# ScalarE reads the decay rate as a scale and takes the decay's square, in the recurrence of the second network

## The reference, cut to what matters

```python
def rg_lru(x, w_r, b_r, w_i, b_i, lam):
    xb = x.reshape(B, S, RNN_BLOCKS, RNN_BLOCK_DIM)
    r = sigmoid(einsum('bsnc,ncd->bsnd', xb, w_r).reshape(B, S, D_RNN) + b_r)
    i = sigmoid(einsum('bsnc,ncd->bsnd', xb, w_i).reshape(B, S, D_RNN) + b_i)
    log_a = -LRU_C * r * softplus(-lam)          # LRU_C = 8
    a = exp(log_a)
    u = sqrt(-expm1(2.0 * log_a)) * (i * x)
    # then h[t] = a[t] * h[t-1] + u[t] along the positions
```

## Time and profile before

| | us |
|---|---|
| median of 3 runs | 2782.74 |
| lowest and highest run | 2771.02, 2784.29 |
| the profiled execution | 2781.65 |
| its span in the profile | 2779.6 |

### The profile page before, as it was taken

The page is one execution under the profiler, slowest core; times in us unless marked ns, Lnnn a source line. Parts: engine busy times, 40 slices in busy tenths (PEclk is TensorE's granted clock), DMA queues, the critical chain, the costliest instruction groups (busy, mean ns, idle before and its releaser), DMA issues. The chain is left out here.

```text
span 2779.6 us, 48273 instructions
## 1 busy us (share of the span) xinstructions
PE 2601.0 (94%) x20505; PEld 2138.3 (77%) x20505; DVE 2017.6 (73%) x2876; ACT 1534.7 (55%) x2217; POOL 128.9 (5%) x176
## 2 busy tenths in 40 slices
PE   8899999998997999999999999998999889999888
PEld 7689987787965666666666666666969779979778
DVE  7755558654356989889898989896757865757864
ACT  5544425221124877777777778775446444546443
POOL 0000000010004000000000000000200101100101
PEclk9999999999997999999999999999999999999999
DMA  6325433100033989899999989893625534625532
GB/s 193 97 73 185 162 117 116 61 4 3 4 135 118 367 331 365 332 347 349 345 351 347 350 330 365 332 365 105 197 74 167 175 104 145 196 76 167 166 105 101
DMA packets 250985, 550.43 MB, mean 198 GB/s; under 512 B 25549, under 2 KB 193157, under 8 KB 207629
## 3 DMA queue, kind: packets, MB, share of 16 engines
q1 hardware_dynamic: 246796, 541.52, 56.1%
q0 software_dynamic: 3968, 5.78, 0.7%
HBM read 540.43 MB, written 1.05 MB: 195 GB/s over the span
## 5 line engine op out<-in xcount | busy, mean ns | idle before, releaser
L316 DVE TENSOR_TENSOR wl<-raw,wh 128x1024 fp32r<-128x1024 f32 (+1 forms) x610 | 742.6, 1221 | 341.8 <-ACT wh L307 324.1
L307 ACT ACTIVATE wh<-raw 128x1024 fp32r<-128x1024 f32 (+1 forms) x610 | 640.5, 1053 | 485.0 <-PE PS L163 434.0
L316 DVE TENSOR_TENSOR wl<-early,wh 128x1024 fp32r<-128x1024 f32 x384 | 466.8, 1225 | 55.6 <-ACT wh L307 35.3
L307 ACT ACTIVATE wh<-early 128x1024 fp32r<-128x1024 f32 x384 | 407.0, 1061 | 128.0 <-PE PS L163 118.7
L161 PE MATMUL PS<-wh,xe_h 128*96 128x512 f32 x896 | 357.2, 399 | 1.2 <-DVE xe_l L2018 1.2
L161 PE MATMUL PS<-b_hn_h,wh 128*128 128x256 f32 (+1 forms) x1152 | 336.9, 292 | 22.1 <-DVE wl L316 15.9
L163 PE MATMUL PS<-wh,xe_l 128*96 128x512 f32 x896 | 353.6, 395 | 0.0
L162 PE MATMUL PS<-wl,xe_h 128*96 128x512 f32 x896 | 353.6, 395 | 0.0
L162 PE MATMUL PS<-b_hn_l,wh 128*128 128x256 f32 (+1 forms) x1152 | 329.6, 286 | 0.0
L163 PE MATMUL PS<-b_hn_h,wl 128*128 128x256 f32 (+1 forms) x1152 | 329.4, 286 | 0.0
L161 PEld LDWEIGHTS PS<-b_hn_h,wh 128*128 128x128 f32 (+1 forms) x1152 | 223.0, 194 | 28.4 <-DVE wl L316 18.3
(11 more groups left out here) (473 smaller groups left out, 5046.8 us busy)
## 6 DMA issues: line engine op xcount, KB each, us to landing
early<-in_moe_in SPq DMA_DIRECT2D x128, 1024.0 KB, 5.0
raw<-in_moe_in SPq DMA_DIRECT2D x96, 1024.0 KB, 4.9
raw<-in_w_in SPq DMA_DIRECT2D x76, 1024.0 KB, 5.4
early<-in_moe_out SPq DMA_DIRECT2D x64, 1024.0 KB, 4.9
raw<-in_moe_out SPq DMA_DIRECT2D x48, 1024.0 KB, 5.0
raw<-in_attn_w_in SPq DMA_DIRECT2D x24, 512.0 KB, 5.8
raw<-in_rw_w_rkv SPq DMA_DIRECT2D x12, 1024.0 KB, 5.0
raw<-in_ffn_w_gate SPq DMA_DIRECT2D x11, 1024.0 KB, 5.5
```

What stands on the lines that cost most here:

```text
L307: act.e.activation(st.two(n)[0], st.raw(n), ACT.Copy).then_inc(*act.sig("hi", st.name, n, sem=f"hi_{st.name}"))
L316: dve.e.tensor_tensor(lo, st.raw(n), hi.bitcast(F32), SUB).then_inc(*dve.sig("lo", st.name, n, sem=f"lo_{st.name}"))
```

## The change

In the stage of bv, VectorE's eight products by the rate are left out. `decays(n)` on ScalarE does the same by its own scale: two exponentials of one block each, with the block's column of nsp as the scale, then two tanh with the column of psp (+8 softplus(-lam), one more small VectorE instruction, put into the scratch column set 4). It waits for the rates and for the gates' eviction. In the stage of mb, the square of the decay moves from VectorE to ScalarE (`squares`), between `high` and the eviction of mb; it waits for its own `decays` and for VectorE's II x CX of the same round, because it overwrites CX. VectorE's `roots_in(n)` comes one round later, behind the next round's II x CX, and the last one after the loop.

```diff
-    nsp = spv[:, 5, :]
+    nsp, psp = spv[:, 5, :], spv[:, 4, :]
@@ second_act
         def decays(n):
+            act.wait_ge(act.at("rates", l))
+            act.wait_ge(act.at("lru", l, 0, 2 * n + 1))
+            for x in (2 * n, 2 * n + 1):
+                e.activation(AA_[:, x, :], RR_[:, x, :], ACT.Exp, scale=nsp[:, x:x + 1]).then_inc(*act.own())
+            act.wait_ge(act.last)
+            for x in (2 * n, 2 * n + 1):
+                e.activation(RR_[:, x, :], RR_[:, x, :], ACT.Tanh, scale=psp[:, x:x + 1]).then_inc(*act.sig("decays", l, n))
+
+        def squares(n):
             c = slice(2 * n, 2 * n + 2)
-            act.wait_ge(act.at("log_a", l, n))
-            e.activation(AA_[:, c, :], RR_[:, c, :], ACT.Exp).then_inc(*act.own())
-            act.wait_ge(act.last)
-            e.activation(RR_[:, c, :], RR_[:, c, :], ACT.Tanh, scale=-1.0).then_inc(*act.sig("decays", l, n))
+            act.wait_ge(act.at("decays", l, n))
+            act.wait_ge(act.at("gated", l, n))
+            e.activation(CX_[:, c, :], AA_[:, c, :], ACT.Square).then_inc(*act.sig("squares", l, n))
...
         for u in range(KC):
             high(act, SB)
+            squares(u)
             taken("mb", u, M[:, u, :], ACT.Sigmoid)
@@ second_dve
-        e.tensor_scalar(nsp_, nsp_, -8.0, None, MUL).then_inc(*dve.own())
+        e.tensor_scalar(psp, nsp_, 8.0, None, MUL)
+        e.tensor_scalar(nsp_, nsp_, -8.0, None, MUL).then_inc(*dve.sig("rates", l))
...
         for u in range(KC):
             low(dve, SB)
-            c = slice(2 * u, 2 * u + 2)
-            dve.wait_ge(dve.at("lru", l, 0, 2 * u + 1))
-            e.tensor_tensor(RR_[:, c, :], RR_[:, c, :], bc(nsp[:, c], [RB, 2, SEQ], 2), MUL).then_inc(*dve.sig("log_a", l, u))
+
+        def roots_in(n):
+            c = slice(2 * n, 2 * n + 2)
+            dve.wait_ge(dve.at("squares", l, n))
+            e.scalar_tensor_tensor(CX_[:, c, :], CX_[:, c, :], 1.0, RR_[:, c, :], ADD, MUL).then_inc(*dve.sig("roots_in", l, n))
+
         for u in range(KC):
             low(dve, SB)
             c = slice(2 * u, 2 * u + 2)
             dve.wait_ge(dve.at("lru", l, 1, NRB - 1))
-            e.tensor_tensor(II_[:, c, :], II_[:, c, :], CX_[:, c, :], MUL).then_inc(*dve.own())
-            dve.wait_ge(dve.at("decays", l, u))
-            dve.wait_ge(dve.last)
-            e.tensor_tensor(CX_[:, c, :], AA_[:, c, :], AA_[:, c, :], MUL).then_inc(*dve.own())
-            dve.wait_ge(dve.last)
-            e.scalar_tensor_tensor(CX_[:, c, :], CX_[:, c, :], 1.0, RR_[:, c, :], ADD, MUL).then_inc(*dve.sig("roots_in", l, u))
+            e.tensor_tensor(II_[:, c, :], II_[:, c, :], CX_[:, c, :], MUL).then_inc(*dve.sig("gated", l, u))
+            if u:
+                roots_in(u - 1)
+        roots_in(KC - 1)
```

More of the change, by code:

```diff
@@ L69 @@
     "route_mm": "by_expert_mm logits_mm ht_mm count_mm rank_mm rows_mm",
-    "b": "iq ik iwt plus plus_exp plus_log xr xr_zero q k iw conv rot spun scored log_a roots_in lru_out rnn_in mb gr ga ma bv lru "
+    "b": "iq ik iwt plus plus_exp plus_log xr xr_zero q k iw conv rot spun scored rates gated squares roots_in lru_out rnn_in mb gr ga ma bv lru "
          "index decays roots",
```

## The result

| | before | after |
|---|---|---|
| median of 8 runs, us | 2781.68 | 2797.19 |
| lowest to highest, us | 2771.02 to 2784.29 | 2793.23 to 2805.89 |
| the profiled execution, us | 2781.65 | 2796.83 |
| its span, us | 2779.6 | 2794.7 |

The ratio is 1.0063, 95% interval 1.0050 to 1.0075: slower, by 15.5 us between the medians.

A forecast was written before the change was run, and what follows sets the result against it. TensorE, busy 94% of the span, was taken as the bound. Layer shifts of 8.8 and 8.1 us, 16.9 together, on the profiled 2781.65 give 2798.5; with 1.1 for the median, 2799.6 us, range 2788 to 2811.

The forecast's parts named there:

- The bound: Whole kernel: TensorE, busy 94% of the span; only what makes it wait, around mb in each layer, moves the time.
- P1 to P9: Weight pieces ScalarE splits, P0 to P7 in mb's eight rounds, P8 and P9 in gr's first; TensorE's 2.86 us each.
- The rate products: bv stretch: removal from VectorE worth nothing; ScalarE's decays 1.73 us, 0.54 more each, 4.3 for eight.
- The lock: mb rounds: ScalarE and VectorE hand over twice a round, 3.74 us against 3.26 before and TensorE's 2.86.
- The sum: Both stretches up to TensorE's start of P9: +8.8 us in layer 1, +8.1 us in layer 2.
- (d): Rival, decays and what follows the stretch: cheaper decays or part of the shift absorbed, 2794.6 us; chance 0.16.
- (a): Rival, mb rounds: they don't lock, TensorE's 4.20 us gap goes, -8.4 in two layers, 2774 us; chance 0.06.
- (b): Rival, mb rounds: Square not in the loaded table set, sigmoids need reloads, 9.7 us a layer, 2819 us; chance 0.04.
- (c): Rival, mb rounds: TensorE's waits drop its clock to 1.2 GHz, 6 us later a layer, 2812 us; chance 0.06.

The follow-up runs named there:

- the experiment: The changed kernel with constants -1 and 1 as the scale of exponentials and tanh in place of rates read from memory: 2794.11 us, ratio 1.0053.

## Why the prediction was right, point by point

**The bound.** The dates that I took as the ones that matter, TensorE's at P1 to P9, are where it waits after the change (all but P2 in layer 1). The parts of the program outside of the two stretches differ between the two executions by 2.3 us at most, and that is ahead of the first stretch.

**The rate products.** Taking them from VectorE was worth nothing, as said: in the regular rounds of bv in layer 1 it stood for ScalarE's high part before (0.3 or 0.8 us) and stands longer now (1.5 or 2.0). Their price on ScalarE was 4.23 us to P0 where I had 4.1, and 3.67 in layer 2 where I had 3.4: a decay took 1.76 us and not 1.73. That forecast and measurement agree within 0.3 us is in part luck, since like kernels differ in P0 by as much and more: over all the runs the price lies between 3.6 and 4.4 us in layer 1 and between 3.4 and 3.7 in layer 2. The activation with the rate took 0.50 us, as worked out from the pair of evictions:

```profile
L2591 ACT ACTIVATE b_aa<-b_rr,b_spv x32: 491/498/511, 2101.4 to 2551.8; 88x256 f32<-88x256 f32 x32
```

The Trainium skill (ScalarE: Activation LUTs, section "What ACT_TABLE_LOAD costs") gives 93 ns for each such operand; the 0.37 us for four in the experiment are that number. What the Trainium skill calls free in the same page's section "Step-by-step: what each stage is for" costs time here.

What I had not seen in full is the way of this delay. The prediction said of a P0 that is ready just before TensorE wants it that nothing is lost up to there, and let the delay cost something only because the locked rounds start with P0. The run with the decays alone shows that P0's delay is paid in full, 3.8 and 3.4 us, without the lock too: VectorE's eight rounds start with the low part of P0 and end with the roots' input.

**The lock.** A round was 3.80 us where I had 3.74. The term that was small is the hand-over from VectorE's product to the square: the product ends at 2125.41 + 0.68 = 2126.09 and the square starts at 2126.18, 0.09, where I had taken 0.03 from the wait before P8. Seven rounds and the last one make 0.5 us: P0 to P8 is 32.37 and not 31.87. The wait of ScalarE is 1.95 each time (forecast 1.9). TensorE's waits are 0.66, where I wrote 0.9 from 3.74 - 2.86: the first matmul behind a wait takes longer (0.39 us in place of 0.28), and the view counts idle time from the end of the last matmul's record. The table load came once, behind the first square, as forecast.

**The sum.** +9.4 and +8.8 were forecast as +8.8 and +8.1, 18.2 against 16.9. The profiled executions differ by 15.2, as the parts outside of the stretches took 3.1 less, 2.3 of them ahead of layer 1, where nothing was changed; the medians differ by 15.5, and 2799.6 stands against 2797.19. Of the 2.4 us between forecast and median, 1.1 are the kernel before, whose median of eight runs lies below that of the first three. The rest is two misses against each other, 1.3 us too little in the stretches and 3.1 outside of them that nobody forecast, so that the median came so near is in part luck. Why the parts outside took 3.1 us less stays open. In the attention behind P9, at least, nothing changed, as (d) shows.

**The rivals.** (a), rounds that don't lock, is not what this order does, and is what the order with the square one round later does: 2775 us against the 2774 that (a) gave. That these are so near is in part chance: (a) wanted the whole gap before P9 gone, 8.4 us, and the trace of that kernel has P9 5.1 us earlier, with 1.64 and 1.47 us of the gap left. (b), reloads of tables: there is one load in the mb rounds of each layer, as before. (c), the clock, came about for a moment. In layer 1, after the 1.78 us that TensorE stood before P1, its clock fell to the lower level, 1.2 GHz, from 2132.18 on:

```profile
2132.18 0.41 PE L163 MATMUL PS<-b_hn_h,wl 128*128 128x256 f32 x1
2132.39 0.41 PE L161 MATMUL PS<-b_hn_h,wh 128*128 128x256 f32 x1
```

```profile
2132.20:2135.40 3.20, 3.20 (x18) 3.20 (x17) 2.12 (x3) 1.25 (x3) 0.00 (x0) 0.50 0.96 311
```

For these 3.2 us the granted clock was 0.50 and matmuls started 0.21 us apart, so P1 took 4.18 us (2130.77 to 2134.95) and not 2.86. P2's low part had been ready at 2134.50; TensorE came 0.45 us late, at the upper level again from 2135.6, and at P3 it waited for VectorE once more, 0.09 us. The slack of the long rounds took it up, and nothing of it reached P9. With the regular waits of 0.66 us the clock stayed at 2.4 GHz, and in layer 2, where the wait before P1 was 1.04 us, it did not fall in the rounds at all. The 6 us a layer that (c) was priced at did not come.

(d), part of the shift absorbed, did not come about: ScalarE's P8 and TensorE's P9 are late by the same (9.38 and 9.39), and from P9 to TensorE's long wait in the attention it is 2217.72 - 2158.53 = 59.19 us before and 2224.79 - 2165.60 = 59.19 after. The first of these rows is of the kernel before, the second of the changed one:

```profile
2217.72 0.48 PE L2491 MATMUL PS<-CB,b_aa 128*128 128x128 f32 x1 [5.46 <-DVE b_aa L2868]
```

```profile
2224.79 0.48 PE L2491 MATMUL PS<-CB,b_aa 128*128 128x128 f32 x1 [5.46 <-DVE b_aa L2879]
```

## What to carry to other kernels

When two engines share a round, write down for each what stands behind its waits: here a square moved "off the busy engine" tied ScalarE's queue to a VectorE result of the same round, and a round took the steps of both engines one behind the other, 3.8 us, in place of the 2.34 us that the busier of the two needs. Placing the wait one round later cost nothing and gave back 22 us. And before shortening the chain that feeds a wait, look at what stands behind the wait without need of it: taking two weight pieces out from behind the roots, with no other edit, gave 9 us, and no version here gained more than 10.

## What the runs showed of the hardware

The hand-over between engines is not one number: a high part behind VectorE's last product started 0.03 us after its end, a square behind VectorE's product 0.09 us, and VectorE's product behind the last square 0.04 (2154.17 + 0.63 to 2154.84). A table load did not wait for what its activation waits for: in the kernel before with the roots later it ran from 2147.93 while the roots' input was still being made (2149.43), so 1.28 us of loading cost nothing there.
